# Decoder layer on one core: the expert stage's row blocks in permuted quarters, transposed by VectorE

## The reference

```python
u = rms_norm(x, norm2_g) * (1.0 + sc2) + sh2
aff = softmax(u @ w_router)              # 16 experts in 4 groups
# best group by the sum of its two best affinities, then the two best experts in it
for e in range(16):
    h = silu(u @ w1[e]) * (u @ w3[e])    # 1024 -> 512
    y = y + gate[:, e:e + 1] * (h @ w2[e])   # 512 -> 1024
x = x + g2 * y
```

## Time and profile before

| | us |
|---|---|
| median of 3 runs (754.96 to 758.34) | 756.02 |
| the profiled execution | 755.66 |
| its span, first to last instruction | 754.0 |
| PE busy (matmul) / weight loads of PE | 613.6 / 362.8 |
| VectorE / ACT / POOL busy | 322.3 / 255.4 / 80.2 |
| HBM read / written | 155.02 MB / 20.71 MB |

### The profile page before, as it was taken

The page is one execution under the profiler, slowest core; times in us unless marked ns, Lnnn a source line. Parts: engine busy times, 40 slices in busy tenths (PEclk is TensorE's granted clock), DMA queues, the critical chain, the costliest instruction groups (busy, mean ns, idle before and its releaser), DMA issues.

```text
span 754.0 us, 15645 instructions
## 1 busy us (share of the span) xinstructions
PE 613.6 (81%) x6231; PEld 362.8 (48%) x6235; DVE 322.3 (43%) x925; ACT 255.4 (34%) x611; POOL 80.2 (11%) x119
## 2 busy tenths in 40 slices
PE   0798999977689988799981388999999999999940
PEld 0544474664356666555440254555555555555520
DVE  3713818233279999933336022232232232222215
ACT  3300200113356677822330143433443343344310
POOL 5001000016100000000002200101110110110022
PEclk9998999989779999999995599999999999999985
DMA  8970957061499300056019649999999999999228
GB/s 326 378 306 7 395 212 276 3 204 30 151 335 216 110 1 1 2 207 240 1 48 350 215 167 363 360 372 361 364 375 359 365 375 361 365 366 362 61 60 302
DMA packets 81389, 176.26 MB, mean 234 GB/s; under 512 B 9410, under 2 KB 26378, under 8 KB 79306
## 3 DMA queue, kind: packets, MB, share of 16 engines
q1 hardware_dynamic: 68592, 152.90, 57.9%
q0 software_dynamic: 8384, 13.97, 5.5%
q10 hardware_dynamic: 4380, 8.94, 3.8%
HBM read 155.02 MB, written 20.71 MB: 233 GB/s over the span
## 4 chain that ended last, share of the span: by engine, by line
PE 25%; DMA 24%; issue 3%; DVE 2%; POOL 2%; ACTq 0%; ACT 0%; POOLq 0%
DMA featT<-expert_rows 22%; PE score L1595 9%; PE score L1495 7%; PE bank L1585 4%; PE score L1604 3%; DMA pool_sb<-expert_rows,idx 1%; POOL pool_sb L805 1%; POOL expert_rows L785 1%; DMA expert_rows<-pool_sb,idx 1%; DMA expert_rows<-featT 1%; PE bank L1530 0%; PE bank L1610 0%; ACTq L680 0%; PE bank L1539 0%; PE bank L1550 0%
## 5 line engine op out<-in xcount | busy, mean ns | idle before, releaser
L1595 PE MATMUL score<-pool_sb,featT 128*32 128x256 f32 x2688 | 162.3, 386 | 20.8 <-DMA featT<-expert_rows 12.1
L1595 PEld LDWEIGHTS score<-pool_sb,featT 128*32 128x32 f32 x2688 | 86.7, 111 | 82.4 <-DMA featT<-expert_rows 26.8
L1291 PE MATMUL bank<-pool_sb,featT 128*128 128x512 f32 (+2 forms) x256 | 88.7, 509 | 5.8 <-DVE featT L860 2.6
L1231 DVE TENSOR_TENSOR featT<-featT,score 128x128 f32<-128x128 f32 x42 | 12.1, 288 | 184.7 <-ACT featT L691 184.7
L1604 PE MATMUL score<-pool_sb,featT 128*32 128x256 f32 x1344 | 82.3, 386 | 0.4 <-ACT featT L696 0.4
L1291 PEld LDWEIGHTS bank<-pool_sb,featT 128*128 128x128 f32 x256 | 49.9, 196 | 43.1 <-issue 35.4
L685 ACT ACTIVATE featT<-bank,mod_col 128x32 f32<-128x32 f32 x129 | 39.4, 375 | 61.2 <-PE bank L1585 61.2
L793 POOL DMA_DIRECT2D expert_rows<-featT x42 | 29.2, 695 | 277.8 <-DVE featT L1227 264.0
L1221 DVE TENSOR_SCALAR featT<-bank,mod_col 128x32 f32<-128x32 f32 x215 | 51.0, 304 | 14.9 <-PE bank L1585 14.9
L1495 PE MATMUL score<-pool_sb,featT 128*128 128x512 f32 x128 | 56.9, 597 | 0.0
L691 ACT ACT_TABLE_LOAD x42 | 53.9, 1283 | 0.8
(11 more groups left out here) (255 smaller groups left out, 679.6 us busy)
## 6 DMA issues: line engine op xcount, KB each, us to landing
pool_sb<-in_moe_w SPq DMA_DIRECT2D x48, 2048.0 KB, 22.2
pool_sb<-in_ada_w SPq DMA_DIRECT2D x16, 1024.0 KB, 7.3
expert_rows<-zeros_f SPq DMA_DIRECT2D x17, 512.0 KB, 6.5
featT<-expert_rows ACTq DMA_DIRECT2D x44, 128.0 KB, 5.4
expert_rows<-featT POOLq DMA_DIRECT2D x42, 128.0 KB, 7.0
pool_sb<-in_ada_w SPq DMA_DIRECT2D x8, 640.0 KB, 11.8
pool_sb<-in_w_out SPq DMA_DIRECT2D x4, 1024.0 KB, 16.7
pool_sb<-in_ada_w SPq DMA_DIRECT2D x8, 384.0 KB, 9.7
```

Of the source, the lines that this page charges most:

```text
L1291: m = nc.tensor.matmul(pj_bank(g, i)[:, 0:n], featT[:, k, i * P:(i + 1) * P], w_stage[:, g % 3, k, 0:n], start=(k == 0), stop=(k == KD - 1))
L1595: mm = nc.tensor.matmul(banks[0][h * BT:(h + 1) * BT, 0:2 * HB], xgT[:, k, :], exp_w13[slot][:, :, k, h * HB:(h + 1) * HB], start=(k == 0) ...
```

## The change

Rows are scattered with their columns permuted: within a row, quarter h holds columns 32h to 32h + 31 of each of the eight chunks of 128 (`x_hat`). A block is loaded as 4 quarters to 4 x 32 partitions, 1 KB each, in two buffers `xg[0]` and `xg[1]`, three blocks ahead. VectorE applies scale and shift there, as two passes with tensors (`scale2_part`, `shift2_part`, built once before the loop), and transposes the 32x32 squares of the 128x256 tile in one instruction, which gives all eight chunks of `xgT`. `hmid` becomes `hT` the same way. For that `inner` takes its quarter h from the weights as columns 32h to 32h + 31 of each of 4 chunks (`w[:, :, :, h, :]`) in place of 128 neighbouring columns. PE's transposes, their evictions on ACT and VectorE, and three semaphores go. ACT keeps the Silu and the loads. PE's stage waits for `m_h` of the block before (bank 0 read) and for `m_xT`. SP issues matrix (2, 0) when the scatter is complete.

```diff
--- before.py
+++ after.py
@@ -76,6 +76,8 @@
         proj = ring[:, 1, 0:TT * N_IN].rearrange("p (i n) -> p i n", i=TT)
         blk = ring[:, 1, TT * N_IN:TT * N_IN + CMP_LEN * KV * NC].rearrange("p (l m) -> p l m", l=CMP_LEN)
         gate2_part = sb("gate2_part", [P, DN])
+        scale2_part = sb("scale2_part", [P, DN])
+        shift2_part = sb("shift2_part", [P, DN])
         gate1_row = sb("gate1_row", [P, D])
         vrow = sb("vrow", [40, P])
         vcol = sb("vcol", [P, 40])
@@ -178,13 +180,20 @@
         block_start = sb("block_start", [1, NE + 3], I32)
 
         blkbuf = featT[:, :, :].rearrange("p k n -> p (k n)")
-        xg = blkbuf[0:BT, 0:D]
-        xgT = blkbuf[:, D:D + KD * BT].rearrange("p (k n) -> p k n", k=KD)
-        silu = blkbuf[:, 2 * D:2 * D + HB]
-        hmid = blkbuf[:, 2 * D + HB:2 * D + 2 * HB]
-        hT = blkbuf[:, 2 * D + 2 * HB:2 * D + 2 * HB + P]
-        y_sb = [blkbuf[:, 3 * D + n * DN:3 * D + (n + 1) * DN] for n in range(2)]
-        y_last = [blkbuf[:, 3 * D + (2 + n) * DN:3 * D + (3 + n) * DN] for n in range(2)]
+        blk_at = [0]
+
+        def blk_view(n):
+            blk_at[0] += n
+            return blkbuf[:, blk_at[0] - n:blk_at[0]]
+
+        xg = [blk_view(DN) for _ in range(2)]
+        xm = blk_view(DN)
+        xgT = blk_view(DN).rearrange("p (k r) -> p k r", r=BT)
+        silu = blk_view(HB)
+        hmid = blk_view(HB)
+        hT = blk_view(HB).rearrange("p (k r) -> p k r", r=BT)
+        y_sb = [blk_view(DN) for _ in range(2)]
+        y_last = [blk_view(DN) for _ in range(2)]
 
         yab = ring[:, :, 0:TT * D].rearrange("p b (i n) -> p b i n", i=TT)
         xs = nc.dram_tensor("expert_rows", (N_ROWS, D), F32, kind="Internal").ap()
...
@@ -470,7 +479,7 @@
             load_matrix(1, 1)
             sp.wait_ge(o_x, 2 * TT)
             load_matrix(2, 2)
-            sp.wait_ge(s_xg, 32)
+            sp.wait_ge(s_scat, 16 * 2 * TT)
             load_matrix(2, 0)
             sp.wait_ge(t_gs, 1)
             for e in range(NE - 3):
@@ -660,7 +669,9 @@
 
             def x_hat(i):
                 act.wait_ge(r_rs, i + 1)
-                nc.scalar.activation(norm_x[:, i, :], x_sb[:, i, :], ACT.Copy, scale=rstd2[:, i:i + 1]).then_inc(r_xh, 1)
+                nc.scalar.activation(norm_x[:, i, :].rearrange("p (h j a) -> p j h a", h=NT, a=BT),
+                                     x_sb[:, i, :].rearrange("p (j h a) -> p j h a", h=NT, a=BT), ACT.Copy,
+                                     scale=rstd2[:, i:i + 1]).then_inc(r_xh, 1)
 
             for j in range(2 * TT):
                 scaled(j)
@@ -676,35 +687,27 @@
             act.wait_ge(r_lm, 1)
             nc.scalar.activation(aff, aff, ACT.Exp).then_inc(r_ex, 1)
 
-            def xg_load(g):
-                act.dma_start(xg, xs[bass.ds(g * BT, BT), :]).then_inc(s_xg, 16)
-
-            def xg_T(g):
-
-                for k in range(3):
-                    m = nc.scalar.activation(xgT[:, 5 + k, :], banks[5][:, k * BT:(k + 1) * BT], ACT.Identity,
-                                             scale=mod_col[:, 21 + k:22 + k], bias=mod_col[:, 29 + k:30 + k])
-                m.then_inc(m_xa, 1)
-
-            def block_of_rows(g):
+            def xg_load(g, n):
+                act.dma_start(xg[n], xs[bass.ds(g * BT, BT), :].rearrange("r (h n) -> h r n", h=NT)).then_inc(s_xg[n], 16)
+
+            def block_of_rows(g, n):
+                act.wait_ge(m_sc, g + 2)
+                xg_load(g + 3, 1 - n)
                 act.wait_ge(m_h1, g + 1)
                 nc.scalar.activation(silu, banks[0][:, 0:HB], ACT.Silu).then_inc(m_si, 1)
-                act.wait_ge(m_xt, g + 2)
-                xg_load(g + 2)
-                xg_T(g + 1)
-                act.wait_ge(m_ht, g + 1)
-                nc.scalar.activation(hT, banks[6][:, 0:P], ACT.Copy).then_inc(m_hT, 1)
 
             act.wait_ge(s_scat, 16 * 2 * TT)
-            xg_load(0)
-            act.wait_ge(m_xt, 1)
-            xg_load(1)
-            xg_T(0)
+            xg_load(0, 0)
+            xg_load(1, 1)
+            act.wait_ge(m_sc, 1)
+            xg_load(2, 0)
             act.wait_ge(t_gs, 1)
-            total = all_blocks(act)
-            with act.Fori(0, total) as g:
-                block_of_rows(g)
-            act.wait_ge(s_xg, total * 16 + 32)
+            pairs = block_pairs(act)
+            with act.Fori(0, pairs) as m:
+                for n in range(2):
+                    block_of_rows(m * 2 + n, n)
+            act.wait_ge(s_xg[0], pairs * 16 + 32)
+            act.wait_ge(s_xg[1], pairs * 16 + 16)
             nc.scalar.activation(ssq2, ssq2, ACT.Copy)
 
         @block.gpsimd
@@ -1215,41 +1218,72 @@
             for b in range(2):
                 ch(nc.vector.tensor_tensor(wab[:, b * TT:(b + 1) * TT], wab[:, b * TT:(b + 1) * TT], wsum, ALU.mult))
 
+            for k0, to in ((16, scale2_part), (24, shift2_part)):
+                nc.vector.tensor_copy(xm.rearrange("p (k r) -> p k r", r=BT), mod_col[:, k0:k0 + KD].unsqueeze(2).broadcast_to([P, KD, BT])).then_inc(m_part, 1)
+                dve.wait_ge(m_part, k0 // 4 - 3)
+                nc.vector.transpose(to[:], xm).then_inc(m_part, 1)
+                dve.wait_ge(m_part, k0 // 4 - 2)
+
+            def rows_in(g, n):
+                dve.wait_ge(s_xg[n], g * 8 + (16 if n == 0 else 8))
+                if not (isinstance(g, int) and g == 0):
+                    dve.wait_ge(m_xT, g)
+                nc.vector.tensor_tensor(xm, xg[n], scale2_part[:], ALU.mult).then_inc(m_sc, 1)
+                dve.wait_ge(m_sc, g + 1)
+                nc.vector.tensor_tensor(xm, xm, shift2_part[:], ALU.add).then_inc(m_mod, 1)
+
             def xg_T(g):
-                dve.wait_ge(m_xt, g + 1)
-                for k in range(5):
-                    m = nc.vector.tensor_scalar(xgT[:, k, :], banks[4][:, k * BT:(k + 1) * BT], mod_col[:, 16 + k:17 + k],
-                                                mod_col[:, 24 + k:25 + k], ALU.mult, ALU.add)
-                m.then_inc(m_xv, 1)
-
-            def rows_out(y, upto):
-                dve.wait_ge(m_y, upto)
+                dve.wait_ge(m_mod, g + 1)
+                nc.vector.transpose(xgT.rearrange("p k r -> p (k r)"), xm).then_inc(m_xT, 1)
+
+            def hmid_T(g):
+                dve.wait_ge(m_h, g + 1)
+                nc.vector.transpose(hT.rearrange("p k r -> p (k r)"), hmid).then_inc(m_hT, 1)
+
+            def rows_out(y):
                 nc.vector.tensor_tensor(y, banks[2][:, 0:DN], gate2_part[:], ALU.mult).then_inc(m_ye, 1)
 
-            def block_of_rows(g):
+            def hidden(g):
+                dve.wait_ge(m_h1, g + 1)
+                xg_T(g + 1)
                 dve.wait_ge(m_si, g + 1)
+                if not (isinstance(g, int) and g == 0):
+                    dve.wait_ge(m_hT, g)
                 nc.vector.tensor_tensor(hmid, silu, banks[0][:, HB:2 * HB], ALU.mult).then_inc(m_h, 1)
-                xg_T(g + 1)
+
+            def block_of_rows(g, n, y):
+                hidden(g)
+                dve.wait_ge(m_y, g)
+                hmid_T(g)
+                rows_out(y)
+                rows_in(g + 2, n)
 
             nc.vector.memset(y_last[0][0:1, 0:1], 0.0).then_inc(m_ye, 1)
+            rows_in(0, 0)
             xg_T(0)
-            block_of_rows(0)
+            rows_in(1, 1)
+            hidden(0)
+            hmid_T(0)
+            rows_in(2, 0)
             dve.wait_ge(t_gs, 1)
             pairs = block_pairs(dve)
             for g in range(1, 3):
-                block_of_rows(g)
-                rows_out(y_sb[(g - 1) % 2], g)
+                block_of_rows(g, g % 2, y_sb[(g - 1) % 2])
             with dve.Fori(1, pairs - 1) as m:
-                block_of_rows(m * 2 + 1)
-                dve.wait_ge(s_ys[0], m * 16)
-                rows_out(y_sb[0], m * 2 + 1)
-                block_of_rows(m * 2 + 2)
-                dve.wait_ge(s_ys[1], m * 16)
-                rows_out(y_sb[1], m * 2 + 2)
-            block_of_rows(pairs * 2 - 1)
+                for n in range(2):
+                    hidden(m * 2 + 1 + n)
+                    dve.wait_ge(m_y, m * 2 + 1 + n)
+                    hmid_T(m * 2 + 1 + n)
+                    dve.wait_ge(s_ys[n], m * 16)
+                    rows_out(y_sb[n])
+                    rows_in(m * 2 + 3 + n, 1 - n)
             last = dve.value_load(block_start[0:1, NE + 2:NE + 3], min_val=MIN_BLOCKS * NE - 1, max_val=MAXB)
-            rows_out(y_last[0], last)
-            rows_out(y_last[1], last + 1)
+            hidden(last)
+            dve.wait_ge(m_y, last)
+            hmid_T(last)
+            rows_out(y_last[0])
+            dve.wait_ge(m_y, last + 1)
+            rows_out(y_last[1])
 
             for i in range(TT):
                 dve.wait_ge(c_g[i], 32)
@@ -1579,20 +1613,12 @@
                     m = nc.tensor.matmul(banks[1][:, o], tri_b[:], mcount[:, o], start=(i == 0), stop=True)
             m.then_inc(r_rank, 1)
 
-            def xg_T():
```

(38 more changed lines are left out.)

## The result

| | median us (runs) | ratio to before, 95% |
|---|---|---|
| before, beside it | 757.18 (754.96 to 759.47) | |
| after | 785.92 (784.04 to 785.97) | 1.0373 [1.0335, 1.0411] |

The change makes the kernel 3.7% slower. The profiled execution took 785.94 us, its span 784.3. The prediction had the direction and the mechanism (771 us, the weight stream held up by the row loads), but its sum is 15 us short: the time lies 2 us above the range for 8 in 10 (738 to 784), and 3 above the forecast's own (757 to 783).

What follows compares the result with a forecast made beforehand. PE was taken as the bound, DMAs close behind; after the change, the weight stream. Stream end 727.5 + 10 behind it + 2 clock = 739.5; + 29.1 + 1.66 + 0.36 = 771 us; range for 8 in 10: 738 to 784.

Steps and rivals of the forecast that it cites:

- PE's block: Expert stage: without PE's transposes a block takes 5.75 us, 1.25 less; VectorE's additions hidden, 32-column groups cost 0.
- What is late next is the weight stream: Expert stage: weights need 19.5 us an expert, PE 15.9, so PE waits for weights and only the stream counts.
- Four engines, the same ones: ACT's row loads: outermost length 4 puts each on the same four DMA engines, 1.7 us each per block.
- Size per expert: Weight stream: row loads add 1.4 to 2.8 us an expert, 2.25 taken, +29 us over 13 experts.
- The start: Start of expert stage: first row load beside matrix (2, 0) costs up to 3.2 us; inner product 0 at 428.8.
- Behind the last matrix, clock, tail: After the stream's end: 10 us of PE products, about 2 for the clock, then the same tail of 29.1.
- 698.0 and 29: End of the weight stream: 698.0 if the stream were unchanged, plus 29 us for the row loads' slowing.
- (a): Rival, row loads: they spread over all engines or rotate, giving 741 us; chance 0.27.
- the store, also on four, slows nothing visibly: Argument for spread loads: the row store, also on four engines, leaves 366 GB/s standing.
- (b): Rival, row loads: their latency binds; at 20 us landing the time is 900 us; chance 0.04.
- (c): Rival, PE: it stays the bound through slower `inner` or late `m_h`; 7.75 us a block, 785 us; chance 0.06.

Runs made afterwards that it cites:

- e8: Kernel before without the weight loads of experts 3 to 15, the first three experts' weights used again; 735.21 us, ratio 0.973.
- e9: Changed kernel without the weight loads of experts 3 to 15, the first three experts' weights used again; 700.28 us, ratio 0.9267.
- e3: Changed kernel with matrix (2, 0) issued only after the first two row loads have landed; 777.38 us, ratio 1.0275.
- e1: Changed kernel with each row load issued as four DMAs of 32 partitions, same bytes and queue; 737.78 us, ratio 0.9738.
- e11: Kernel before with each row store issued as four DMAs of outermost length 32; 749.24 us, ratio 0.9897.
- e2: Changed kernel with its row loads, same pattern, issued by POOL instead of ACT, one block earlier; 767.77 us, ratio 1.0143.
- e6: Changed kernel with row loads issued by POOL, each as four DMAs of outermost length 32; 740.83 us, ratio 0.9775.
- e10: Changed kernel with row loads and row stores each as four DMAs, and matrix (2, 0) after the first two row loads; 725.43 us, ratio 0.9578.

## Why the prediction was right in direction and short in size

- *PE's block.* Forecast 5.75, measured 5.18 to 5.45. PE is not the bound, so it changed nothing. VectorE's work, ACT's, and the groups of 32 columns cost nothing on the path (once the stage runs, PE waits for VectorE 2.9 us in all), as forecast.
- *What is late next is the weight stream.* Right: 68.6 us of weight waits, and e8 and e9 turn the sign round by taking the stream away.
- *Four engines, the same ones.* Right: 4 completions a load, 0.2 of the engines for 7 us at the end, a lag of 11.0. That they are the same four each time is seen in e3, where two loads pass one behind the other over four engines, and in the four late completions of matrix after matrix, which are gone with POOL issuing (8.2 us against 1.4). The sentence of the Trainium skill that ACT's go to the lowest-numbered and GpSimd's rotate (DMA: Bandwidth & Descriptors, Why a DMA increments its semaphore by 16 and not by 1) fits that, but which engines they are no run shows.
- *Size per expert: the first failed term.* Taken +2.25, bounded at +1.4 to +2.8; measured +3.12, above the upper end. The step that failed is "with the other engines partly idle the packets may run faster": over the stage they took 47.2 us per MB, not 41.7 to 45.0. They do run faster where 12 engines are idle (39.5 from 738 to 744), but the stage as a whole got slower packets, not faster ones. With that number, (0.393 x 47.2 + 2.625 x 1.66) / 1.05 + 1.1 gives 22.9 (the load's 1.66 is 5.1% x 3520 / 27 loads / 4), against 22.62 measured; the form of the sum was sound, the packet time was not. The 47.2 is a mean over all 16 engines, and what it was on the busy four isn't shown, so that the sum comes within 0.3 is partly luck. Over 13 experts 294.0 instead of 282.5: +11.5.
- *The start: the second failed term.* "Up to 3.2 us" for a row load beside matrix (2, 0) was taken from the loads under a running stream; beside a matrix issued in the same instant it was 9.5 against 2.1, so 7.4, of which 5.5 fall to the matrix and 1.9 to the new pattern. Inner product 0 at 435.13 instead of 428.8, the release of (3, 0) at 451.07 instead of 445: +6.0. e3 measures the start at 8.5, the noise of two comparisons included.
- *Behind the last matrix, clock, tail.* 10.4 for 10; the 2 us for the clock weren't paid, as the inner product at 739.47 (5.75, at the lower of the two clock levels: the granted clock is 0.50 in the window shown above) ran while w2's last engines were still at work; the tail 0.3 shorter.
- *The sum.* 11.5 + 6.0 + 0.4 - 2 - 0.3 = 15.6; 785.9 - 770.3 = 15.6. Three slips in the recorded sum don't matter beside that: the middle of 1.4 and 2.8 is 2.1, not 2.25; 698.0 and 29 make 727.0, not 727.5; and its own upper terms (37, 10 and 4) end at 780, not 783.
- *Rivals.* (a) spread loads, 741: not what happened, but e1 builds just that and took 737.78, so the price on that side was right, with some luck: its stream is 18.94 us an expert, not 19.5, and matrix (3, 0) goes out at 449.1, not 445. Its argument "the store, also on four, slows nothing visibly" was false: it cost 8 us (e11). (b) and (c): no row wait of PE once the stage runs, and an inner product takes 3.64 at full clock. Some are slower at the lower clock after a weight wait, as at 739.47; PE isn't the bound, so it isn't on the path.
- *The range* erred in one way twice: both upper bounds came from rows of the kernel before, with its load spread evenly over the engines, and neither was a bound of the changed one.

Open: why weight packets take longer while rotating groups of four load rows (48.4 us per MB in e2, 44.7 in e6), with the share at 1.05 in both; why some of them take much longer in the changed kernel while half of them don't; and how much of either goes with the size of the row packets, which changes with the pattern.

## What to carry to other kernels

When the 16 engines are nearly full, a small DMA that only four of them serve puts four times the work on each of these four, and every large transfer that needs all sixteen waits for them. Here it was split so that the outermost length of each part is 32 and not 4. Look at the last digits of a DMA row (all at once, or a tail of 0.2). A gain of 35 us on the compute side became a loss of 29; the shape of 128 KB a block accounts for 48 us between the two, the start for 6 to 9. Issue the small load that starts a pipeline and let it land before the big one that nobody waits for yet.

## What the runs showed of the hardware

- Weight packets took 47.2 us per MB on average with 12 engines partly idle, 45.0 before, 43.4 in e1 and 42.1 in e10 with the small transfers over all engines. Where four engines alone were at work (738 to 744) they took 39.5.
- Two loads of outermost length 4 in flight on ACT's queue kept 0.2 to 0.3 of the engines busy (e3, 424.5 to 427.5), and the second finished on each of its four engines 1.36 to 1.37 us behind the first.
- 128 KB of rows issued beside 2 MB of weights on another queue landed after 9.5 us; the same load with the matrix held back after 4.0 (e3), and in the old pattern alone after 2.1.
- VectorE transposes the 32x32 squares of a 128x128 tile of float32 in 311 ns, of 128x256 in 445 ns. The Trainium skill (VectorE: DVE Perf Modes, The three transpose paths) has 311 ns for 128x128 in bf16; here float32 took the same.
- A moving operand in groups of 32 columns costs no more than 128 neighbouring ones: 64 products in 3.64 us against 3.66.
- ACT loads its table 21 times for 42 blocks, 1283 ns each, though Silu is its only function in the loop: once for each pass of a loop body that holds two blocks. Before, with one block a pass and other functions in it, there were 42.
